# A decoder block on one core: four high-half buffers with the low half in place, and the state space running sums spread from HBM scratch

## What is computed

```python
u = n @ w_in
y_a = short_conv_mixer(u_a, conv_a_w) @ w_branch_a
y_b = stick_breaking_attention(u_b) @ w_branch_b
y_c = mamba2_ssd(u_c, ...) @ w_branch_c
h = x + (g_a * y_a + g_b * y_b + g_c * y_c) @ w_out
```

```python
da = dt * a                                   # per head and token
a_cs = jnp.cumsum(da, axis=-1)                # within a chunk
y_diag = einsum(cb, segsum_exp(da), xdt)      # segsum_exp: exp(a_cs[l] - a_cs[s]), l >= s, else 0
y_off  = einsum(cm, prev, jnp.exp(a_cs))
```

## Time and profile before

| | |
|---|---|
| median of 3 runs | 3591.6 us (3589.92 to 3593.02) |
| the profiled execution | 3588.55 us |
| its span in the trace | 3586.8 us |
| TensorE busy | 3486.1 us, 97% |
| DVE busy | 2281.0 us, 64% |
| ACT busy | 1726.7 us, 48% |
| DMA | 620.2 MB, 173 GB/s on average |
| TensorE clock granted | 0.998 |
| first ring, from first split to last | 17 to 1936 us of the span |

### The profile page before, as it was taken

One profiled execution on the slowest core, in us unless ns is written; L12 is line 12 of the kernel. 1 busy time (PEld: TensorE's weight loads), 2 busy tenths in 40 slices (PEclk: granted clock), 3 DMA queues, 4 the chain that ended last, 5 costly groups with the idle time before them and its releaser, 6 DMA issues.

```text
span 3586.8 us, 70545 instructions
## 1 busy us (share of the span) xinstructions
PE 3486.1 (97%) x23289; PEld 3182.5 (89%) x23289; DVE 2281.0 (64%) x2908; ACT 1726.7 (48%) x2502; POOL 27.5 (1%) x32
## 2 busy tenths in 40 slices
PE   8999999999999999999999989999999999999998
PEld 8998789988799999987778989899999988887887
DVE  4555444444447777774455899988888855554555
ACT  4444444444434544554445434447777644444444
POOL 0000000000000000000000000000000000000000
PEclk9999999999999999999999999999999999999999
DMA  6666665556665554546677567676666677667665
GB/s 187 178 176 174 188 177 148 146 145 171 189 190 155 154 154 146 156 137 181 185 214 205 149 156 170 158 181 162 159 159 159 161 195 193 193 192 217 194 193 166
DMA packets 482778, 620.20 MB, mean 173 GB/s; under 512 B 76640, under 2 KB 341184, under 8 KB 481472
## 3 DMA queue, kind: packets, MB, share of 16 engines
q1 hardware_dynamic: 482624, 618.14, 64.2%
HBM read 613.64 MB, written 4.19 MB: 172 GB/s over the span
## 4 chain that ended last, share of the span: by engine, by line
PE 83%; DVE 8%; ACT 3%; issue 2%; DMA 2%; SPq 1%; DVEq 0%; ACTq 0%
PE bank L79 27%; PE bank L81 26%; PE bank L80 26%; PE bank L1693 3%; DMA w_raw<-in_peer_down 2%; DVE w_lo L1539 2%; PE bank L2114 2%; DVE f_lo L128 2%; ACT f_hi L123 2%; DVE w_raw L1532 1%; SPq L527 0%; DMA w_raw<-in_peer_up 0%; DVE g_sig L1269 0%; ACT c_xpad L684 0%; DVE t_cand L1474 0%
## 5 line engine op out<-in xcount | busy, mean ns | idle before, releaser
L128 DVE TENSOR_TENSOR f_lo<-f_raw,f_hi 128x768 fp32r<-128x768 f32 (+2 forms) x640 | 748.8, 1171 | 782.1 <-ACT f_hi L123 781.7
L123 ACT ACTIVATE f_hi<-f_raw 128x768 fp32r<-128x768 f32 (+2 forms) x640 | 649.8, 1016 | 894.6 <-PE bank L81 891.0
L79 PE MATMUL bank<-xT_hi,f_hi 128*128 128x256 f32 x2560 | 742.7, 290 | 36.4 <-DVE f_lo L128 21.8
L80 PE MATMUL bank<-xT_lo,f_hi 128*128 128x256 f32 x2560 | 723.5, 283 | 0.0
L81 PE MATMUL bank<-xT_hi,f_lo 128*128 128x256 f32 x2560 | 723.4, 283 | 0.0
L79 PE MATMUL bank<-xT_hi,w_hi 128*128 128x256 f32 x2048 | 590.7, 288 | 21.7 <-DVE w_lo L1539 21.6
L80 PE MATMUL bank<-xT_lo,w_hi 128*128 128x256 f32 x2048 | 579.0, 283 | 0.0
L81 PE MATMUL bank<-xT_hi,w_lo 128*128 128x256 f32 x2048 | 578.8, 283 | 0.0
L79 PEld LDWEIGHTS bank<-xT_hi,f_hi 128*128 128x128 f32 x2560 | 488.8, 191 | 52.0 <-DVE f_lo L128 28.5
L1631 DVE TENSOR_TENSOR w_lo<-w_raw,w_hi 128x1024 fp32r<-128x1024 f32 x256 | 313.7, 1225 | 342.1 <-PE bank L81 335.0
L80 PEld LDWEIGHTS bank<-xT_lo,f_hi 128*128 128x128 f32 x2560 | 489.7, 191 | 1.9 <-issue 1.7
(11 more groups left out here) (268 smaller groups left out, 4922.2 us busy)
## 6 DMA issues: line engine op xcount, KB each, us to landing
w_raw<-in_peer_down SPq DMA_DIRECT2D x1024, 128.0 KB, 3.6
w_raw<-in_peer_up SPq DMA_DIRECT2D x1024, 128.0 KB, 2.7
f_raw<-in_w_in SPq DMA_DIRECT2D x1024, 96.0 KB, 2.4
f_raw<-in_w_in SPq DMA_DIRECT2D x256, 256.0 KB, 2.9
f_raw<-in_w_in SPq DMA_DIRECT2D x384, 128.0 KB, 2.8
f_raw<-in_w_branch_c SPq DMA_DIRECT2D x256, 128.0 KB, 2.7
f_raw<-in_w_branch_a SPq DMA_DIRECT2D x128, 128.0 KB, 2.7
f_raw<-in_w_branch_b SPq DMA_DIRECT2D x128, 128.0 KB, 2.8
```

Of the source, the lines that this page charges most:

```text
L79: nc.tensor.matmul(out, lhs[0], rhs[0], start=start, stop=False, skip_group_check=True)
L80: nc.tensor.matmul(out, lhs[0], rhs[1], start=False, stop=False, skip_group_check=True)
L123: nc.scalar.activation(self.hi[u % 2][:, 0:cols], self.raw[u % 4][:, 0:cols], ACT.Copy).then_inc(self.hi_done, 1)
L128: nc.vector.tensor_tensor(self.lo[u % 2][:, 0:cols], self.raw[u % 4][:, 0:cols], self.hi[u % 2][:, 0:cols].bitcast(F32), ALU.subtract).the ...
```

## The change

Two changes. **The ring:** the low half is written over the raw data, in the same slot; the freed space gives high halves four buffers, like raw. The wait for use moves from `split_hi` (ACT, unit n-2) to `room` (SP, unit n-4), where it takes the place of the wait for the low half. **The running sums:** `diffs` and the c_dag copy are gone. Two float32 matmuls in `dt_step` (m = 23) make the running sums of all 64 heads, one chunk each, as 64 rows; DVE copies them to cs_row (m = 26); SP, after the loads of the conv stage's branch, waits for them and stores them to the HBM scratch in eight DMAs, one a group, each 8 heads by 2 chunks of 128 values. In the state space stage SP issues one load a group, behind the load of unit 4 of the next group, that reads the group's 2048 values and spreads them over 128 partitions straight into c_wts (1 MB written). `clamp` subtracts in place in c_wts; `exp_cs` reads chunk 1 of c_wts, moves from u = 13 to u = 9, and becomes one operation of 1024 columns; the clamp of chunk 1 waits for it. The copy to c_prev stays at u = 13.

```diff
@@ class Flow
-                self.hi = [place(f"f_hi{i}", [P, SLOT // 4], at_ring + (4 + i) * SLOT, F32R) for i in range(2)]
-                self.lo = [place(f"f_lo{i}", [P, SLOT // 4], at_ring + (6 + i) * SLOT, F32R) for i in range(2)]
+                self.lo = [place(f"f_lo{i}", [P, SLOT // 4], at_ring + i * SLOT, F32R) for i in range(4)]
+                self.hi = [place(f"f_hi{i}", [P, SLOT // 4], at_ring + (4 + i) * SLOT, F32R) for i in range(4)]
...
             def room(self, sp, n):
                 if not (isinstance(n, int) and n < 4):
-                    sp.wait_ge(self.lo_done, n - 3)
+                    sp.wait_ge(self.used, n - 3)
...
                 act.wait_ge(self.raw_full[u % 4], (quads + u // 4 + 1) * 64)
-                if not (isinstance(n, int) and n < 2):
-                    act.wait_ge(self.used, n - 1)
@@ SP
                 branch_load(GA0, COL_G, w_branch_a, KD)
+                sp.wait_ge(d_rows, 1)
+                for g in range(GROUPS):
+                    sp.dma_start(cs_rows[g, 0, :, :, :].rearrange("c h l -> h c l"),
+                                 cs_row[HPG * g:HPG * g + HPG, :].rearrange("h (c l) -> h c l", c=TB)).then_inc(d_vec, 16)
...
+                def cs_load(p):
+                    if not first_p(p):
+                        sp.wait_ge(ssd["y"], 2 * p)
+                    sp.dma_start(wts[:, :, :, :].rearrange("p c h l -> p (c h l)"),
+                                 cs_rows[ds(p, 1), 0, :, :, :].rearrange("o c h l -> o (c h l)").to_broadcast([P, TB * HPG * P])
+                                 ).then_inc(ssd["cs_in"], 16)
+
+                sp.wait_ge(d_vec, 48 + 16 * GROUPS)
+                for u in range(UN):
+                    c_load(C0 + u, 0, u)
+                with sp.Fori(1, N_IT) as it:
                     for u in range(UN):
                         c_load(C0 + UN * it + u, it, u)
+                        if u == 4:
+                            cs_load(it - 1)
+                branch_load(GC0, COL_G + 2 * D, w_branch_c, KC, 4)
@@ GpSimd, ACT
-                    pool.wait_ge(ssd["ecs"], 2 * p + 2)
+                    pool.wait_ge(ssd["ecs"], p + 1)
...
                 def exp_cs(p):
-                    for q in range(2):
-                        act.wait_ge(ssd["sub"], 4 * p + 2 + q + 1)
-                        nc.scalar.activation(ce[:, 4 * q:4 * q + 4, :],
-                                             bank[5 + q][:, :].rearrange("p (h l) -> p h l", h=4),
-                                             ACT.Exp).then_inc(ssd["ecs"], 1)
+                    act.wait_ge(ssd["cs_in"], 16 * p + 16)
+                    nc.scalar.activation(ce[:, :, :], wts[:, 1, :, :], ACT.Exp).then_inc(ssd["ecs"], 1)
...
+                        if u == 9:
+                            exp_cs(p)
                         if u == 13:
-                            exp_cs(p)
+                            copy_prev(p)
@@ DVE
+                        nc.vector.tensor_copy(cs_row[0:H, :], bank[7][0:H, P:P + T]).then_inc(d_rows, 1)
...
-                    nc.vector.tensor_copy(dag[:, :, :], da[:, :, here]).then_inc(ssd["dag"], 1)
...
                 def clamp(p, ch):
+                    if ch == 0:
+                        dve.wait_ge(ssd["cs_in"], 16 * p + 16)
+                    else:
+                        dve.wait_ge(ssd["ecs"], p + 1)
                     for q in range(2):
-                        dve.wait_ge(ssd["diff"], 4 * p + 2 * ch + q + 1)
                         nc.vector.tensor_tensor(
-                            wts[:, ch, 4 * q:4 * q + 4, :], bank[5 + q][:, :].rearrange("p (h l) -> p h l", h=4),
+                            wts[:, ch, 4 * q:4 * q + 4, :], wts[:, ch, 4 * q:4 * q + 4, :],
@@ TensorE
+                        for ch in range(TB):
+                            last = mm(bank[7][0:H, (1 + ch) * P:(2 + ch) * P], da[:, ch, :], upper[:, :], False)
+                        last.then_inc(d_proj, 1)
...
-                    for q in range(2):
-                        for h in range(4):
-                            last = mm(bank[5 + q][:, h * P:(h + 1) * P], bcast(ch, 4 * q + h), upper[:, :], h == 0)
-                        last.then_inc(ssd["diff"], 1)
...
-                    if u == 8:
-                        diffs(p, 0)
-                    if u == 10:
-                        diffs(p, 1)
```

More of the change, by code:

```diff
@@ L115, in room @@
                 if not (isinstance(n, int) and n < 4):
-                    sp.wait_ge(self.lo_done, n - 3)
+                    sp.wait_ge(self.used, n - 3)
             def split_hi(self, act, n, quads, u, cols):
                 act.wait_ge(self.raw_full[u % 4], (quads + u // 4 + 1) * 64)
-                if not (isinstance(n, int) and n < 2):
-                    act.wait_ge(self.used, n - 1)
-                nc.scalar.activation(self.hi[u % 2][:, 0:cols], self.raw[u % 4][:, 0:cols],
+                nc.scalar.activation(self.hi[u % 4][:, 0:cols], self.raw[u % 4][:, 0:cols],
                                      ACT.Copy).then_inc(self.hi_done, 1)
@@ L127, in split_lo @@
                 dve.wait_ge(self.hi_done, n + 1)
-                nc.vector.tensor_tensor(self.lo[u % 2][:, 0:cols], self.raw[u % 4][:, 0:cols],
-                                        self.hi[u % 2][:, 0:cols].bitcast(F32),
+                nc.vector.tensor_tensor(self.lo[u % 4][:, 0:cols], self.raw[u % 4][:, 0:cols],
+                                        self.hi[u % 4][:, 0:cols].bitcast(F32),
                                         ALU.subtract).then_inc(self.lo_done, 1)
@@ L243, in program @@
         d_out = sem("d_out")
+        d_rows = sem("d_rows")
         W, UN, N_IT = 1280, 16, GROUPS
@@ L258, in program @@
         b_tok = place("c_b_tok", [P, P], at_s + 43136)
-        dag = place("c_dag", [P, TB, HPG], at_s + 43648)
+        cs_row = place("cs_row", [P, T], at_s + 4096)
+        cs_rows = h_dram.rearrange("(g o) (c h l) -> g o c h l", o=T // GROUPS, c=TB, h=HPG)
         ssd = {n: sem("c_" + n) for n in (
-            "pad", "evac", "conv", "xc", "tr", "btok", "cbm", "xdt", "dag", "diff", "sub", "min", "exp", "wts",
+            "pad", "evac", "conv", "xc", "tr", "btok", "cbm", "xdt", "cs_in", "sub", "min", "exp", "wts",
             "zs", "cs", "ecs", "prev", "ce", "y", "skip", "yz", "sq", "fold", "sum", "rs", "yn", "yhi", "ylo")}
@@ L470, in c_load, with branch_load @@
                         sp.dma_start(dst, src).then_inc(fl.raw_full[u % 4], 16)
-                def branch_load(base, gate_col, w_branch, kb):
+                def branch_load(base, gate_col, w_branch, kb, cs_at=None):
                     for seg, kind, p, u, m in walk(kb):
+                        if m == cs_at:
+                            cs_load(N_IT - 1)
                         if kind == "g":
@@ L1752, in b_unit @@
                         tri_matmul(bank[m // 2][:, (m % 2) * T:(m % 2 + 1) * T],
-                                   (fl.hi[u % 2][:, at], fl.lo[u % 2][:, at]), xs,
+                                   (fl.hi[u % 4][:, at], fl.lo[u % 4][:, at]), xs,
                                    start=u == 0 and m % 2 == 0, stop=u == KD - 1)
@@ L1760, in b_unit @@
                         last = tri_matmul(V[:, tb * T:(tb + 1) * T], (xT_hi[:, u, t], xT_lo[:, u, t]),
-                                          (fl.hi[u % 2][:, at], fl.lo[u % 2][:, at]),
+                                          (fl.hi[u % 4][:, at], fl.lo[u % 4][:, at]),
                                           start=u == 0 and tb == 0, stop=u == KD - 1)
@@ L1912, in branch_unit @@
                                    (yT_hi[:, y0 + k, t], yT_lo[:, y0 + k, t]))
-                            last = tri_matmul(bank[pair[tb]][:, :], lhs, (fl.hi[m % 2][:, at], fl.lo[m % 2][:, at]),
+                            last = tri_matmul(bank[pair[tb]][:, :], lhs, (fl.hi[m % 4][:, at], fl.lo[m % 4][:, at]),
                                               start=k == 0, stop=k == (KD if kind == "g" else kb) - 1)
@@ L1954, in _ @@
                             pe.wait_ge(d_out, 2)
+                            pe.wait_ge(d_rows, 1)
                     if kind == "b" and p == 0:
```

15 lines of the change are left out of this document (3 added, 12 removed).

## The result

The changed kernel takes **3543.14 us**, the median of four executions (3538.37 to 3548.14), against 3590.76 (3586.07 to 3593.02) for the kernel before: a ratio of 0.9871, with a 95% interval of 0.9856 to 0.9887. The profiled execution took 3542.42 us, 46.1 us less than the one of before. The forecast was 3570, with a range from 3546 to 3592.

The account below looks back on a forecast made before the run. TensorE, busy 97% of the span, was taken to bound the kernel. The terms summed to -21.2 us, which from the profiled 3588.55 us plus 3.05 us gave 3570 us, range 3546 to 3592.

Parts of the forecast that it names:

- Removed matmuls, -27.2: State space groups: 16 stretches of running-sum matmuls of 1.70 us leave TensorE uncovered, saving 27.2 us.
- GpSimd's block, +15: State space unit 9: GpSimd's moved multiplication blocks DVE, 2.2 us for each of 8 groups less 2.6 us, +15 us.
- rival 1: GpSimd's block is hidden, so its +15 us falls away: 3555 us, chance 0.20.
- Attention, -19.5 and +5: Attention stage: gaps before units 7, 8 and 13 go, 2.8 us a turn, seven turns, -19.5; late landings +5 us.
- Conv, +4: Conv stage: with less room in the ring, late loads and small DMAs holding up SP cost 4 us.
- Branches, -5: The same chain once in the branch stage following attention, and short gaps after the gates, go: -5 us.
- Spreading load, 0: State space stage: the 1 MB load issued after load 4 is hidden, 0 us, up to +10.
- Eight stores, +1: Row stores ahead of the first attention loads take 3.7 us of SP, mostly covered: +1 us, bounds 0 and 3.7.
- Output projection, +5: Loads behind the 2 MB re-read of x leave a gap near 4 us, others smaller: +5 us, bounds 0 and 8.
- Rivals 2, 3 and 4: 2: slow spreading load, 3588 us, 0.10; 3: starving ring, 3610 us, 0.12; 4: DVE sets the pace, 3590 us, 0.08.

Follow-up runs that it names:

- ring_only: The kernel before with the ring's part of the change alone, running sums staying on TensorE: 25.5 us faster than before, which took 3589.78 us.
- early_small: The changed kernel with the conv stage's seven small DMAs all issued at u = 3: no gain, conv stage 293.1 us.
- after_again: The changed kernel run once more, unaltered, as yardstick: conv stage 292.5 us, output projection 101.0 us.
- x_parts: The changed kernel with the 2 MB re-read of x cut into four quarters spread over the output projection: 3538.97 us.
- early_x: The changed kernel with the seven small conv DMAs issued at u = 3 and the re-read of x in four parts: 10.4 us below the changed kernel.
- after_nomul: The changed kernel with GpSimd multiplying only 8 of the 1024 columns of c_ce: median moved by 2 us, ranges overlapping.

## Why the prediction was right and wrong

- **Removed matmuls, -27.2:** nearly right in size, but only beside the new ring: -22.6 in the stage, whose seven groups are 23.8 of the term. With the old ring -15.0. The eighth group, in the branch, brought 0.6 us at most. I let ring and sums stand as separate terms; the chain through the high half of unit 10 ties them, and a cover that goes must be asked for on every later unit, not for the block alone. The tie went unpriced and did no harm, since the change has both.
- **GpSimd's block, +15: the step that failed.** That it moves, onto xdd, and its 2 us were right; what it costs TensorE was not. I took the places of ACT and DVE from the trace of before, in which the high halves were still gated by TensorE, and GpSimd's 2.72 us from rows in which it starts 0.5 us before the end of a low half. I put the end of the low half of unit 9 at 10.6 us after `turn` starts (1248.5 less 1237.9); it ends 8.8 us after it, and TensorE wants it at 8.6. GpSimd starts 1.2 us earlier in the group than I had it and takes 2.40 us. But for these 2 us this is rival 1, to which I gave only 0.20 because "three operations with two SBUF inputs follow at once": they do, but only one of them pays, and the others run when GpSimd is done. Measured: 0.37 us a group, 4 to 6 us in the traces and 2 in the medians. That is 9 to 13 of the 27 us by which the forecast was off; attention (6), the branches (6) and the untouched rest (4) brought most of the others.
- **Attention, -19.5 and +5:** the gaps before units 7, 8 and 13 went. A later turn fell from 43.0 to 39.9 us, 3.1 where 2.8 was forecast, and the seven turns after the first by 20.5 us together. The +5 for late landings was mis-sized: 2.3 us in the first turn, and no wait for f_lo from 610 us on.
- **Conv, +4:** the number holds, by luck in part. It was to be landings that are late once in a while in every round; it lies in the first two rounds alone, and 3.7 us of it in the first, beside the small DMAs, which I had priced at 1.4 us.
- **Branches, -5:** in ring_only the three are 5.1, 3.6 and 8.4 us shorter, 17 in all; I counted chains after the gates in one of them. Where the 17 us come from was not taken apart. The changed kernel gives back part (11.2 us stay), in its trace 3.7 us by the block in the last group.
- **Spreading load, 0:** right, with little to spare. Eight stores, +1: not tried apart; they take SP 2.75 us where 3.7 was reckoned, and the last unit before attention and its first are 3.0 us apart, where they are 2.7 in ring_only.
- **Output projection, +5:** mis-sized. The gap came (5.75 us for 4), the half clock behind it was not in the sum; measured +7.3.
- **Rivals 2, 3 and 4** fell: no gap at units 5 or 6, no starving (landing median 2.3 us, where 2.7 was the point), and DVE doesn't set the pace of the stage.
- **The range** ended at 3546, rival 1 with every landing on time (3555 - 9). It was missed by 3 us; the branches alone brought 6 us more than their term, and no bound was set for that term.

What stays open: what sets off the half-clock stretches in the untouched rest, which differs by up to 7 us between executions, and the late load of early_small. A version with the multiplication on another engine, and one with the eight stores elsewhere, were not tried.

## What to carry to other kernels

A cost that hangs on which of two operations comes first must be placed on a timeline redrawn for the new order: when a gate goes, everything behind it moves, and here 1.8 us of shift turned 15 us of forecast loss into 2 to 6. When instructions leave the bounding engine, follow every chain that ran in their shadow; two parts of a change can be worth more together (47 us) than apart (38). And a large one-time load beside a ring just deep enough belongs in parts: here it cost its gap and then the slower clock behind it.

## What the runs showed of the hardware that was not expected

- **A gap costs twice.** Behind the 5.75 us gap TensorE was granted 0.5 of its clock, 1.2 of 2.4 GHz, for 6.8 us; behind two of 2.07 and 2.73 us in the last group, for 3.4 us. early_small had 3.4 us of it behind a gap of 1.91 us in conv, and after_again, x_parts and early_x behind a single one of 2.1 us in the last group. The length of the gap alone doesn't decide: after_nomul had one of 2.73 us in the last group and kept 1.0. Attention's former gaps of up to 1.12 us left it at 1.0.
- **Twice the size, half as long again.** A DMA of 192 KB landed 3.4 us after its issue and one of 96 KB 2.3 us, with the same queue and kernel otherwise.
- **The block falls on whoever comes first.** The same multiplication lengthened c_wts by 2.2 us in the kernel before (2884 against 684 ns), c_xdd by 1.94 us in six groups of the one after (2624 against 680) and two low halves by 1.92 us in another (4.80 against 2.88), one operation each time; the PSUM reader that overlapped its start kept its time. It works the other way too: in the second group of the changed kernel, the first that has one, GpSimd's operation started just after a low half of 1.48 us and took 3.72 us in place of 2.40.
